# Issue of the key and value pages in a decoder step: two of four pages by ScalarE, two by SyncE

## The chip, the core and the metric

The kernel runs on one core of a Trainium2 chip. The metric is device time in microseconds (us), from the launch of the program to its end, of one execution; the median of several executions is given. Engines are called PE (TensorE, matrix products), DVE (VectorE), ACT (ScalarE), POOL (GpSimd) and SP (SyncE, which only issues DMAs here). Each has its own instruction queue, which it works off in order.

## What is computed

The reference is one inference step of a two-layer hybrid decoder: a prompt of 1024 tokens and 8 samples of 4 new tokens go through the same weights. Each layer runs an SSD scan, a sparse attention and a convolution beside one another, then an output projection, a norm and a gated FFN. The change concerns the attention of the samples. Each sample has 2048 past keys in 16 pages of 128 rows, which lie scattered in a pool and are found through a page table:

```python
def sparse_attend(q, ks, vs, valid):
    s = jnp.einsum('bthd,btkhd->bthk', q, ks).astype(jnp.float32) * HEAD_DIM ** -0.5
    s = jnp.where(valid[:, :, None, :], s, -jnp.inf)
    p = jax.nn.softmax(s, axis=-1).astype(vs.dtype)
    return jnp.einsum('bthk,btkhd->bthd', p, vs)
...
        phys = jnp.take_along_axis(page_table, (pi // PAGE_SIZE).reshape(bsz, -1), axis=1).reshape(idx.shape)
        off = pi % PAGE_SIZE
...
        def pick(cache, new):
            old = cache[phys, layer, off].astype(new.dtype)
            return jnp.where(in_past[..., None, None], old, gather_rows(new, ni))

        return sparse_attend(q, pick(cache_k, k), pick(cache_v, v), valid)
```

The kernel doesn't gather rows. It loads every page of keys and of values, scores all keys, and masks those that the indexer has not chosen.

## The kernel before

Each layer runs the same stages, one after the other: projections and the indexer, the SSD scan with the scoring of the sample's past keys woven into it (the key stage below), the attention of the prompt with the weighing of the sample's past values woven into it (the value stage is its later part), then output projection, norm and FFN. A stage ends with all engines waiting for one another.

**Pages and groups.** 8 samples x 16 pages are 128 pages for keys and as many for values. They are loaded in groups of four pages (one page of each of four samples), `STREAM` = 32 groups a layer for keys and 32 for values. A page is 128 x 256 float32, 128 KB. A group fills one of `NSLOT` = 4 slots of the ring `RING`; the slot's semaphore counts to 64, 16 for each page, and PE waits for all four. The list `LOADS` gives the order in which weights, keys and values go through the four slots.

**Who issues.** `load_pages(eng, layer, name, pages_of_group)` loads, for each page, its number out of the page table into a register of the issuing engine's sequencer (L424) and issues the DMA (L425). SP walks through `LOADS`; before each it waits until the slot is free (`k_used` or `v_used`, raised by PE after the last product with a group), then calls `load_pages` for its share. Of the first four groups of keys it loads all four pages, of all others pages 0, 1 and 2. ACT loads page 3 of the others, at places written out by hand in its own program:

- in the key stage, `key_tick(k)`: PE turns half a group of keys (two pages, L935) in each tick and scores a group (L947) at the end of each second one; ACT copies each turned half from PSUM into the slot (L1252), and at each odd tick, after its copy, issues the page for the group `k // 2 + 2`. Eight ticks, so four groups, follow in each of eight chunks of the scan; between these bursts lie the scan's own products and the eight exponentials of L1474.
- at the start of the attention stage, for the first four groups of values, before anything else.
- in the value stage: attention runs in pairs of heads, p = 0 to 17. In step p PE makes the scores of pair p (L1084), weighs the three groups of values that `values_of_pair(p)` names (L1159, from p = 7 on), turns the probabilities of the two blocks of pair p - 1 (L1094) and weighs pair p - 2 (L1107). ACT in the same step runs the two exponentials of pair p (L1488), copies the two turned blocks of pair p - 1 (L1252, copy A and copy B below), and then issues the page for each of the groups four further on. DVE masks the scores (L2077) ahead of the exponentials and takes the reciprocal of the sums (L2067) behind them.

In the first pairs, DVE adds the indexer's choice to the sample's scores in turn with PE (L2105 and L1122); these additions stand in DVE's queue between the masks and the reciprocals.

Of the kernel before, what the change touches and what calls it, by code (L numbers as in the profile page):

```python
# [95 lines left out]
NSLOT = 4  # L96
# [82 lines left out]
def build(nc, xT, w_in, w_out, w_up, w_down, vec, ln0, const, pages, cache_k, cache_v, cache_kidx,  # L179
          ssm_in, ssd_in, cc_in, ffn_in, yT, kT_out, v_out, ki_out, ssm_p, ssm_s, ssd_out, cc_out, ffn_out):  # L180
    ctx = ExitStack()
    with ctx:
# [234 lines left out]
        def load_pages(eng, layer, name, pages_of_group):  # L417

            kind, g = name
            cache = {"key": cache_k, "value": cache_v}[kind]  # L420
            w = 256
            for j in pages_of_group:
                at_page = (4 * (g // PAGES) + j) * PAGES + g % PAGES
                page = eng.value_load(PT[0:1, at_page:at_page + 1], min_val=0, max_val=cache_k.shape[0] - 1)  # L424
                eng.dma_start(RING[:, SLOTS[name], j * w:(j + 1) * w], cache[page, layer, :, :]  # L425
                              ).then_inc(loaded[SLOTS[name]], 16)
# [106 lines left out]
        def _(sp):  # L533
# [7 lines left out]
            with sp.Fori(0, DEPTH) as layer:  # L541
# [17 lines left out]
                for n, name in enumerate(LOADS):  # L559
                    kind, slot = name[0], n % NSLOT  # L560
                    if name == ("kidx", 6):
                        sp.wait_ge(stage_done, 4 * 1)
                        store(ki_out[layer, :, :], KID[0:HEAD, :])
                    elif name == ("key", NSLOT):
                        sp.wait_ge(saved, 8)
                        store(ssd_out[layer, :, :, :], SSDO[:, :, :])
                        store(cc_out[layer, :, :, :], CCO[:, :, :])
                        sp.wait_ge(stage_done, 4 * 3)
                        sp.dma_start(HS[:, :, :, :], ssm_in[layer, :, :, :, :]).then_inc(ssm_loaded, 16)
                        for t in range(2):  # L570
                            store(kT_out[layer, t, :, :], KTL[:, t, :])
                        store(v_out[layer, 0:P, 0:NCHUNK, :], VTOK[:, 0:NCHUNK, :])
                        store(v_out[layer, 0:NS, NCHUNK, :], VTOK[0:NS, NCHUNK, :])
                    elif name == ("value", NSLOT):
                        sp.wait_ge(ssd["state"], NCHUNK)
                        store(ssm_p[layer, :, :, :], HP[:, :, :])
                        sp.wait_ge(ssd["state"], NCHUNK + 1)
                        store(ssm_s[layer, :, :, :, :], HS[:, :, :, :])
                    if name == ("up", NSLOT - WHOLE):
                        sp.wait_ge(stage_done, 4 * 5)  # L580
                        for i, j in enumerate(BY_THIRD):
                            sp.dma_start(WOUT[:, i, :], w_out[layer, j, :, :]).then_inc(wout_loaded[i], 16)
                        sp.dma_start(FFO[:, :, FFN_H:], ffn_in[layer, :, :, :]).then_inc(hist_loaded, 16)
                    if n >= NSLOT:
                        old = LOADS[n - NSLOT]
                        if old[0] in ("in", "out", "up", "down"):
                            await_full(sp, JOB[old])
                        elif old[0] == "value":
                            sp.wait_ge(v_used, old[1] + 1)
                        elif old[0] == "key":  # L590
                            sp.wait_ge(k_used, old[1] + 1)
                        else:
                            sp.wait_ge(tr_full, 4 * old[1] + 4)
                    if kind == "kidx":
                        load_index_pages(sp, layer, name[1], 0, 16)
                    elif kind in ("key", "value"):
                        load_pages(sp, layer, name, (0, 1, 2, 3) if kind == "key" and name[1] < NSLOT else (0, 1, 2))
                    elif kind == "in":
                        sp.dma_start(RING[:, slot, 0:KT * P], w_in[layer, name[1], :, :]).then_inc(loaded[slot], 16)
                    elif kind == "out":  # L600
                        sp.dma_start(RING[:, slot, 0:KT * P], w_out[layer, name[1], :, :]).then_inc(loaded[slot], 16)
                    elif kind == "up":
                        sp.dma_start(RING[:, slot, 0:KT * P], w_up[layer, name[1], :, :]).then_inc(loaded[slot], 16)
                    else:
                        first, w = name[1] * FG * P, split_width(name) * P
                        sp.dma_start(RING[:, slot, 0:w], w_down[layer, name[2], :, first:first + w]
                                     ).then_inc(loaded[slot], 16)
# [641 lines left out]
        def _(act):  # L1249
# [85 lines left out]
            with act.Fori(0, DEPTH) as layer:  # L1335
# [112 lines left out]
                def key_tick(k):  # L1448
                    if k < 2 * STREAM:
                        copy_keys(k)  # L1450
                    g = k // 2 - 1
                    if k % 2 and g >= 0 and (g + 1) % 4 == 0 and g < STREAM:
                        quad, q = divmod(g // 4, QUARTERS)
                        act.wait_ge(k_used, g + 1)
                        copy(PAST[quad][:, q * QKEYS:(q + 1) * QKEYS], bank(7)).then_inc(k_kept, 1)
                    if k in FRESH_TICKS:
                        act.wait_ge(k_fresh, FRESH_TICKS.index(k) + 1)
                        copy(FRESH[:, FRESH_TICKS.index(k), :], bank(7, NS)).then_inc(k_kept, 1)
                    ahead = k // 2 + 2
                    if k % 2 and NSLOT <= ahead < STREAM:  # L1460
                        act.wait_ge(k_used, ahead - NSLOT + 1)
                        load_pages(act, layer, ("key", ahead), (3,))

                act.wait_ge(ssd["seg"], 1)
                act.activation(WS[:, 0:NCHUNK, :], WS[:, 0:NCHUNK, :], ACT.Exp)
# [52 lines left out]
                        copy(PRT[0:NS, PAGES, :].rearrange("p (b x) -> p b x", x=16), src).then_inc(smp["copied"], 1)  # L1518

                for g in range(NSLOT):  # L1520
                    load_pages(act, layer, ("value", g), (3,))
                for p in range(len(BLOCKS) // 2 + 1):
                    for n in (2 * p, 2 * p + 1):
                        if n < len(BLOCKS):
                            exp(n)
                    if p == TURNED_AT - 1:
                        exp_sample()
                    for m in turns_of_pair(p):
                        copy_sample(m)
                    if p >= 1:  # L1530
                        copy_turned(2 * p - 2)
                        copy_turned(2 * p - 1)
                    for g in values_of_pair(p):
                        if g + NSLOT < STREAM:
                            act.wait_ge(v_used, g + 1)
                            load_pages(act, layer, ("value", g + NSLOT), (3,))
                stage.end()


# [29 lines left out]
                for m in range(WHOLE, len(SPLIT)):  # L1569
                    name = SPLIT[m]  # L1570
# [869 lines left out]
```

## Time and profile before

| | |
|---|---|
| median of 3 runs | 3820.9 us (3813.37 to 3825.1) |
| the profiled execution | 3816.51 us, its span 3814.7 us |
| busy share PE, DVE, ACT, POOL | 87%, 50%, 32%, 17% |
| key stage, first and second layer | about 586 to 745 and 2460 to 2617 us |
| value stage, first and second layer | about 872 to 981 and 2743 to 2855 us |

Times in the rows are us from the span's start, unless marked ns. A `q` behind an engine (SPq, ACTq) means its sequencer: issuing of DMAs and loads of registers, which don't count as busy time. The chain of work that ended last is followed back from the last instruction, at each step to what released it. The two layers run the same code, and most rows of the first have a counterpart some 1872 us later.

### The profile page before, as it was taken

What the parts mean: (1) busy time and instruction counts of PE and PEld (TensorE: products, weight loads), DVE (VectorE), ACT (ScalarE), POOL (GpSimd) and SP (SyncE); (2) the same over time, 40 slices, a digit from 0 to 9 for tenths busy, and PEclk for the clock granted to TensorE, in tenths of its full rate; (3) what the DMA queues carried; (4) which work ended last, traced back from release to release, by engine and by line L of the source; (5) the groups of instructions that cost most, each with busy time, mean ns of one, the idle gap of its engine ahead of it and who ended that gap; (6) DMA issues with size and microseconds to landing.
All of it is one profiled execution on the core that took longest, in us unless ns stands there. A gap on an engine that the chain in (4) does not pass through costs nothing.

```text
span 3814.7 us, 51646 instructions
## 1 busy us (share of the span) xinstructions
PE 3304.1 (87%) x19286; PEld 2652.2 (70%) x19286; DVE 1909.9 (50%) x2976; ACT 1236.7 (32%) x2251; POOL 638.6 (17%) x651
## 2 busy tenths in 40 slices
PE   4899887857889999999868998786669999999995
PEld 2454455624789999999834453564349899999994
DVE  4467864332475434334435868633226645335335
ACT  3246623333252112212223574243333412112213
POOL 0000000001013333333100000000110333334331
PEclk8999998857999999999989998897589999999998
DMA  3111104304301111111021110142151111111111
GB/s 100 49 36 29 32 17 124 94 17 123 102 17 35 52 48 37 53 50 34 27 81 48 34 34 23 62 117 63 35 155 40 34 45 36 54 45 37 55 34 58
DMA packets 169894, 206.59 MB, mean 54 GB/s; under 512 B 61025, under 2 KB 138146, under 8 KB 168738
## 3 DMA queue, kind: packets, MB, share of 16 engines
q1 hardware_dynamic: 143138, 185.36, 16.4%
q10 hardware_dynamic: 26496, 17.84, 1.6%
q8 instruction: 154, 2.52, 0.3%
q14 instruction: 106, 0.87, 0.1%
HBM read 187.17 MB, written 15.96 MB: 53 GB/s over the span
## 4 chain that ended last, share of the span: by engine, by line
PE 64%; DVE 16%; ACT 9%; SPq 5%; issue 3%; DMA 2%; POOL 0%; ACTq 0%; DVEq 0%; POOLq 0%
PE PS L742 41%; PE PS L723 7%; DVE WORK L1668 4%; DVE MIX L1668 2%; ACT WORK L1435 2%; PE PS L755 2%; PE PS L827 2%; ACT X L1306 2%; SPq L424 2%; SPq L425 2%; DVE WORK L1860 1%; PE PS L935 1%; DMA RING<-cache_k 1%; PE PS L781 1%; DVE WORK L1632 1%
## 5 line engine op out<-in xcount | busy, mean ns | idle before, releaser
L742 PE MATMUL PS<-WORK_parts,WHIGH_parts 128*128 128x352 f32 x4224 | 869.5, 328 | 35.2 <-POOL WORK_parts L709 17.7
L723 PE MATMUL PS<-X,RING 128*128 128x512 f32 (+1 forms) x2016 | 671.8, 496 | 109.3 <-DMA RING<-w_in 65.4
L742 PEld LDWEIGHTS PS<-WORK_parts,WHIGH_parts 128*128 128x128 f32 x4224 | 724.2, 191 | 38.9 <-issue 20.6
L742 PE MATMUL PS<-WORK_parts,RING_parts 128*128 128x352 f32 x3168 | 691.3, 327 | 0.0
L723 PEld LDWEIGHTS PS<-X,RING 128*128 128x128 f32 x2016 | 338.4, 194 | 443.8 <-issue 375.2
L742 PEld LDWEIGHTS PS<-WORK_parts,RING_parts 128*128 128x128 f32 x3168 | 545.4, 190 | 0.0
L1668 DVE SCALAR_TENSOR_TENSOR WORK<-WORK,VEC 128x1072 f32<-128x1072 f32 (+2 forms) x272 | 525.6, 1932 | 9.7
L1252 ACT ACTIVATE WORK<-PS 128x32 f32<-128x32 f32 (+11 forms) x412 | 190.8, 514 | 842.1 <-PE PS L742 579.7
L489 POOL TENSOR_TENSOR RING_parts<-RING,WHIGH_parts 128x1024 fp32r<-128x1024 f32 (+2 forms) x184 | 372.0, 2022 | 467.2 <-ACT WHIGH_parts L1252 466.9
L742 PE MATMUL PS<-X_parts,WHIGH_parts 128*128 128x352 f32 x2016 | 434.4, 323 | 0.0
L1435 ACT ACTIVATE WORK<-WORK 128x512 bf16<-128x512 f32 x310 | 285.7, 922 | 198.5 <-DVE WORK L1907 198.4
L1666 DVE TENSOR_SCALAR WORK<-WORK,VEC 128x1072 f32<-128x1072 f32 (+2 forms) x102 | 80.0, 784 | 529.8 <-ACT WORK L1252 529.4
L742 PEld LDWEIGHTS PS<-X_parts,WHIGH_parts 128*128 128x128 f32 x2016 | 344.4, 188 | 0.0
L1252 ACT ACTIVATE WHIGH_parts<-RING 128x1024 fp32r<-128x1024 f32 (+2 forms) x188 | 155.5, 827 | 442.6 <-PE PS L742 420.0
L2264 DVE TENSOR_TENSOR MIX<-MIX,PS 128x1056 f32<-128x1056 f32 x80 | 100.3, 1253 | 286.9 <-PE PS L742 286.9
L755 PE MATMUL PS<-WORK_parts 128*128 128x352 f32 x576 | 144.2, 330 | 0.0
L2077 DVE CUSTOM_DVE_ANT_0 WORK<-PS,WORK 128x384 f32<-128x384 f32 (+5 forms) x48 | 42.4, 883 | 201.8 <-PE PS L1084 201.8
L709 POOL TENSOR_TENSOR WORK_parts<-WORK,WORK_parts 128x1056 fp32r<-128x1056 f32 x44 | 108.3, 2462 | 167.6 <-ACT WORK_parts L1252 167.6
L1252 ACT ACTIVATE WORK_parts<-WORK 128x1056 fp32r<-128x1056 f32 (+1 forms) x56 | 59.4, 1078 | 217.9 <-DVE WORK L2252 217.9
L935 PE MATMUL PS<-CONST,RING 128*128 128x128 f32 x512 | 83.0, 305 | 49.5 <-DMA RING<-cache_k 30.7
L1860 DVE TENSOR_SCALAR_CACHE_REDUCE WORK<-WORK 128x544 bf16<-128x544 f32 (+6 forms) x164 | 115.9, 742 | 0.3
L935 PEld LDWEIGHTS PS<-CONST,RING 128*128 128x128 f32 x512 | 62.3, 155 | 67.9 <-DMA RING<-cache_k 37.0
(318 smaller groups left out, 3722.2 us busy)
## 6 DMA issues: line engine op xcount, KB each, us to landing
RING<-w_up SPq DMA_DIRECT2D x88, 512.0 KB, 3.6
RING<-cache_k SPq DMA_DIRECT2D x200, 128.0 KB, 2.2
RING<-cache_v SPq DMA_DIRECT2D x192, 128.0 KB, 2.1
RING<-w_in SPq DMA_DIRECT2D x46, 512.0 KB, 3.6
RING<-w_down SPq DMA_DIRECT2D x80, 256.0 KB, 2.7
RING<-cache_v ACTq DMA_DIRECT2D x64, 128.0 KB, 2.5
RING<-cache_k ACTq DMA_DIRECT2D x56, 128.0 KB, 2.6
yT<-X SPq DMA_DIRECT2D x5, 1408.0 KB, 5.5
```

The costliest lines, as they stand in the source:

```text
L489: eng.tensor_tensor(low, raw, WHIGH[:, m % 2, 0:w].bitcast(F32), ALU.subtract).then_inc(done, 1)
L709: pool.tensor_tensor(HIDL[:, b, :], HID[:, b, :], HIDH[:, b, :].bitcast(F32), ALU.subtract).then_inc(hid_low, 1)
L723: mm = pe.matmul(job_psum(n, w, first=first), stationary(k), moving(k)[:, first:first + w], start=k == 0, stop=k == k_tiles - 1)
L742: mm = pe.matmul(thirds(n)[:, third, :], a, x[:, third * THIRD:(third + 1) * THIRD], start=k == 0 and part == 0, stop=k == tiles - 1 and p ...
L755: mm = pe.matmul(dst, a[:, w], third_of(x, t), start=k == 0 and part == 0, stop=k == KT - 1 and part == 2)
L935: mm = pe.transpose(key_bank(k)[:, (j % 2 * 2 + t) * P:(j % 2 * 2 + t + 1) * P], cache_page(name)[:, j, t * P:(t + 1) * P], c("ident"))
L1252: return act.activation(dst, src, ACT.Copy)
L1435: ins = act.activation(SCAN_ASIDE[s][:, 0:w], SEL[:, SEL_AT[i]:SEL_AT[i] + w], ACT.Sign, bias=SCAN_TRIED[:, s:s + 1], scale=SCAN_SCALE, ac ...
L1666: step.then_wait(dve.tensor_scalar(acc, src[:, 0:w], v(col), None, ALU.mult))
L1668: ins = dve.scalar_tensor_tensor(out=acc, in0=src[:, k:k + w], scalar=v(col + k), in1=acc, op0=ALU.mult, op1=ALU.add)
L1860: marks.append(step.mark(dve.tensor_scalar(ASIDE[len(marks) % 2][:, 0:x.shape[-1]], x, limit, None, op, ALU.add, accum_out=to)))
L2264: dve.tensor_tensor(y, y, thirds(n), ALU.add).then_inc(free[n % 2], 1)
```

## The change

SP issues pages 0 and 1 of each group in place of 0, 1 and 2; ACT issues pages 2 and 3 in place of page 3, at the same places of its program. The first four groups of keys stay with SP alone. What is loaded, where to, and what waits for it stay as they are.

```diff
@@ -594,7 +594,7 @@
                     elif kind in ("key", "value"):
-                        load_pages(sp, layer, name, (0, 1, 2, 3) if kind == "key" and name[1] < NSLOT else (0, 1, 2))
+                        load_pages(sp, layer, name, (0, 1, 2, 3) if kind == "key" and name[1] < NSLOT else (0, 1))
@@ -1459,7 +1459,7 @@
                     if k % 2 and NSLOT <= ahead < STREAM:
                         act.wait_ge(k_used, ahead - NSLOT + 1)
-                        load_pages(act, layer, ("key", ahead), (3,))
+                        load_pages(act, layer, ("key", ahead), (2, 3))
@@ -1518,7 +1518,7 @@
                 for g in range(NSLOT):
-                    load_pages(act, layer, ("value", g), (3,))
+                    load_pages(act, layer, ("value", g), (2, 3))
@@ -1533,7 +1533,7 @@
                         if g + NSLOT < STREAM:
                             act.wait_ge(v_used, g + 1)
-                            load_pages(act, layer, ("value", g + NSLOT), (3,))
+                            load_pages(act, layer, ("value", g + NSLOT), (2, 3))
```

## Rows read from the trace of the kernel before

**Rows 1.** The page: its first line, and the engines' shares of the chain.
```profile
span 3814.7 us, 51646 instructions
...
PE 64%; DVE 16%; ACT 9%; SPq 5%; issue 3%; DMA 2%; POOL 0%; ACTq 0%; DVEq 0%; POOLq 0%
```
**Rows 2.** The page's DMA issues: count, KB each, median us from issue to landing.
```profile
RING<-cache_k SPq DMA_DIRECT2D x200, 128.0 KB, 2.2
RING<-cache_v SPq DMA_DIRECT2D x192, 128.0 KB, 2.1
...
RING<-cache_v ACTq DMA_DIRECT2D x64, 128.0 KB, 2.5
RING<-cache_k ACTq DMA_DIRECT2D x56, 128.0 KB, 2.6
```
**Rows 3.** The chain in the first layer's value stage: start, us, what.
```profile
880.23 0.33 SPq L425
...
942.02 0.33 SPq L425
...
964.80 3.06 DMA RING<-cache_v
...
972.62 4.15 DMA RING<-cache_v
```
**Rows 4.** Timeline of PE in one burst of keys: start, us, what, [idle before <-releaser].
```profile
656.44 1.09 PE L935 MATMUL PS<-CONST,RING 128*128 128x128 f32 x8 [2.02 <-DMA RING<-cache_k]
...
658.39 1.09 PE L935 MATMUL PS<-CONST,RING 128*128 128x128 f32 x8 [0.28 <-DMA RING<-cache_k]
```
**Rows 5.** Timeline of ACT in the same burst.
```profile
653.65 0.37 ACTq L425 DMA_DIRECT2D RING<-cache_k  x1
654.07 1.08 ACT L1252 ACTIVATE RING<-PS 128x512 f32<-128x512 f32 x2 [0.58 <-PE PS L935]
654.88 0.36 ACTq L425 DMA_DIRECT2D RING<-cache_k  x1
```
**Rows 6.** Timeline of ACT in the first layer's value stage (L1488 exponential, L1252 copy).
```profile
874.61 0.60 ACT L1252 ACTIVATE WORK<-PS 128x512 f32<-128x512 f32 x1 [0.81 <-PE PS L1094]
...
883.79 0.60 ACT L1252 ACTIVATE WORK<-PS 128x512 f32<-128x512 f32 x1 [3.80 <-PE PS L1094]
885.66 0.60 ACT L1252 ACTIVATE WORK<-PS 128x512 f32<-128x512 f32 x1 [1.27 <-PE PS L1094]
...
890.88 0.83 ACT L1488 ACTIVATE WORK<-WORK 128x640 f32<-128x640 f32 x1 [4.62 <-DVE WORK L2077]
...
895.05 0.70 ACT L1252 ACTIVATE WORK<-PS 128x640 f32<-128x640 f32 x1 [0.92 <-PE PS L1094]
...
950.89 0.92 ACT L1252 ACTIVATE WORK<-PS 128x896 f32<-128x896 f32 x1 [1.91 <-PE PS L1094]
...
957.78 1.16 ACT L1488 ACTIVATE WORK<-WORK 128x1024 f32<-128x1024 f32 x1 [5.96 <-DVE WORK L2077]
...
960.13 1.00 ACT L1252 ACTIVATE WORK<-PS 128x1024 f32<-128x1024 f32 x1
962.73 1.02 ACT L1252 ACTIVATE WORK<-PS 128x1024 f32<-128x1024 f32 x1 [1.60 <-PE PS L1094]
963.49 2.63 ACTq L425 DMA_DIRECT2D RING<-cache_v  x3
...
971.86 1.02 ACT L1252 ACTIVATE WORK<-PS 128x1024 f32<-128x1024 f32 x1 [1.25 <-PE PS L1094]
```
**Rows 7.** Timeline of ACT at the start of the first layer's attention.
```profile
797.46 3.74 ACTq L425 DMA_DIRECT2D RING<-cache_v  x4
...
802.53 0.40 ACT L1488 ACTIVATE WORK<-WORK 128x128 f32<-128x128 f32 x1
```
**Rows 8.** Timeline of DVE at the same place.
```profile
805.59 0.69 DVE L2105 TENSOR_TENSOR WHIGH<-WHIGH,PS 128x512 f32<-128x512 f32 x1 [1.64 <-PE PS L1122]
```
**Rows 9.** Timeline of ACT in the second layer's value stage: first and last copy B.
```profile
2748.78 0.60 ACT L1252 ACTIVATE WORK<-PS 128x512 f32<-128x512 f32 x1 [0.81 <-PE PS L1094]
...
2844.16 1.02 ACT L1252 ACTIVATE WORK<-PS 128x1024 f32<-128x1024 f32 x1 [1.25 <-PE PS L1094]
```

## The prediction, made before the changed kernel was run

> **What bounds the kernel now.** I read the chain of work that ended last first. TensorE carries 64% of it and the issuing of DMAs by SP 5% [rows 1], about 190 us, unusual for an engine that computes nothing. The list of issues says which DMAs those can be: pages of the key and value caches, 200 and 192 on SP, 56 and 64 on ACT, all of 128 KB [rows 2]. The chain in order of time shows where the issuing is late. In the value stage of the first layer SP issues 53 pages from 880.23 to 942.02 us, 61.79/52 = 1.19 us each, and the chain hardly leaves it [rows 3]: three pages a group, 3.6 us a group. There SP's queue sets the pace.
>
> In the key stage the chain runs through SP only in short pieces. Each SSD chunk turns and scores four groups of keys, which I call a, b, c, d. TensorE waits 2.02 us for c at 656.44 and 0.28 us for d at 658.39 [rows 4]. What releases c is ACT's page of it, issued at 653.65 and needed 2.7 us later [rows 4, 5]; what releases d is SP's third page. Seven chunks of each layer, the second to the eighth, repeat this.
>
> **ACT's price.** Where ACT issues three pages in a row it takes 2.63 us from the first to the end of the third, whose own issue is 0.37 long, so (2.63 - 0.37)/2 = 1.13, say 1.14 us, a page [rows 6]: the load of the page number and its checks are in it, and it is as dear as on SP. The change moves 28 key and 32 value pages a layer, 120 in all, 137 us of issuing. SP gives them up, ACT takes them. On ACT they stand in program order between the copies and exponentials that TensorE and VectorE wait for, so everything queued behind them starts later unless it was waiting anyway.
>
> **Keys.** ACT issues its page of c in the tick in which it copies a, and its page of d one tick later; between the two lies 654.88 - 653.65 = 1.23 us, with the copies of b between [rows 5]. With two pages each, c's last page goes at 653.65 + 1.14, d's first at 653.65 + 1.14 + 1.23 = 656.02 and d's last at 657.16. All land about 2.7 us after issue (656.39 - 653.65; the medians of all pages are 2.6 on ACT, 2.2 on SP [rows 2]). So c comes 1.14 us later, plus 0.1 as more pages are in flight; d comes at 659.9 in place of 658.35, 1.5 us later. SP's release is worth nothing here: its third page of d is replaced by one of ACT that goes later still, and its pages for the next chunk are landed before that chunk starts. Per chunk I count 1.5 us where d's landing ended the wait, four of seven in each layer, and 1.2 where TensorE is still busy with c when d comes, three of seven: 8 x 1.5 + 6 x 1.2 = 19.2 us. I take 2 off, since in some chunks a landing was slower than the rest now, and a later issue need not repeat that: 17 us. Ends: 14 (c alone, 1.0 a chunk) and 25 (1.8 a chunk). The other groups' second page, and the copies that it holds back, lie under the 8 us of SSD work between two bursts: nothing, and 1.14 us each if that cover went.
>
> **Start of the attention stage.** ACT first issues one page of each of the first four groups of values, four in 3.74 us from 797.46, and only then the first exponential, at 802.53 [rows 7]. Eight pages put it at 802.53 + 4 x 1.14 = 807.1, its end with the read of the sum at 807.6. VectorE's reciprocal waits for that, and behind the reciprocal in its queue is the addition at 805.59 [rows 8], which now waited for TensorE. It moves to 807.8: 2.2 us, and the additions after it follow one another with TensorE, so the 2.2 stay. Two layers: 4.4 us. Ends: 0 and 2 x 4.56 = 9.1.
>
> **Values.** A step of this stage is, on ACT: two exponentials, copy A, copy B, three groups' pages. From copy B's start to its first page 0.76 us pass (963.49 - 962.73) [rows 6]. Six pages then hold ACT for 0.76 + 5 x 1.14 + 0.37 = 6.83, with the hand-over 6.86 us after copy B began; now it is 3.4. The exponentials were waiting for VectorE's masks until then: they started 5.22 us after copy B at 890.88, and none later than 957.78 - 950.89 = 6.9 [rows 6]. So ACT's slack of up to 3.4 us is used up, and ACT sets the step: 6.86, plus the two exponentials (960.13 - 957.78 = 2.35 at 1024 keys; by their widths 1.75 at 640, mean 2.05), plus copy A to copy B (1.87 in the first of eight steps, 2.60 in the last [rows 6]; all eight add up to 17.5 in the first layer, 18.6 in the second). Eight steps: 8 x (6.86 + 2.05) + 17.5 = 88.8 us. The ninth has no exponentials; its third group needs ACT's fourth page, issued 0.76 + 3 x 1.14 after copy B and landing 2.7 later, at 962.73 + 6.9 = 969.6 in place of SP's 967.86 [rows 3, 6], so it takes 9.13 + 1.7 = 10.8. Together 99.6 against 971.86 - 874.61 = 97.25 now: 2.4 us. The last group's second page adds 1.14 at the very end, where the chain waits for that landing [rows 3]: 3.5 us. The second layer in the same way: 8 x 8.91 + 18.6 + 10.8 = 100.7 against 2844.16 - 2748.78 = 95.38 [rows 9], 5.3 + 1.14 = 6.5 us. Sum 10 us. Ends: 3.9, if all eight pairs of copies take 1.87, and 15.5, if all take 2.60; below nothing in the second rival.
>
> SP's seven remaining microseconds a step are under ACT's; a value group's slot is freed by TensorE as before, and SP no longer is late for it. What SP issues next, the output weights, waits for the same release as now. VectorE's and GpSimd's steps wait for ACT or TensorE and only follow.
>
> **A rule of the skill.** What the rows say is that 1.19 us of issuing stands against 2.2 us to landing, and that SP is on the chain for 60 us [rows 2, 3]. The Trainium skill, "DMA: Bandwidth & Descriptors", section "Issuing engines are not separate DMA queues", says that issuing from several engines saves only the sequencer's time, which is usually small beside the DMA. Here the trace does not agree that it is small. By that rule nothing would move and the time would stay at 3821; this stands as a rival below.
>
> **The sum.** 17 + 4.4 + 10 = 31.4 us. The profiled execution took 3816.5 us, of which 3814.7 is its span [rows 1]; with the change 3847.9. It lies 4.4 below the median of the runs, 3820.9, to which the same sum gives 3852.
>
> **The rivals.** First, not slower: SP's queue is the bound of the value stage and ACT's pages stay hidden there. It decides at 6.86 us after copy B: if the masks come later than that, ACT's issuing costs nothing. Steps as short as 895.05 - 885.66 = 9.4 occur now [rows 6]; at 9.6 eight steps take 76.8 instead of 88.1, 22.6 us less over two layers. With 21.4 for the other two places this ends at 3821 - 1 = 3820. Against it: most masks come before 6.86 already. 10%. Second, the same with the keys' pages hidden as well, as would be if c and d waited for SP alone: 3820.9 - 22.6 + 4.4 = 3803; the row at 656.44 speaks against it. 4%. Third, slower still: pages of both queues, issued in step, delay one another. The last value page took 4.15 us to land [rows 3]; were all last pages of c and d as late, 1.4 us more in 14 chunks, 20 us, give 3872. Most land in 2.7. 9%. Fourth, issuing is small and nothing moves: 3821. 3%; the 53 pages in the chain speak against it.
>
> **How the numbers follow.** My forecast, 3852, has 74%. Its own range, from the low ends (14 + 0 + 3.9 = 18) to the high ones (25 + 9.1 + 15.5 = 50), is 3839 to 3871. The range to be given reaches down towards the first rival and up to the third: 3828 to 3873. A measurement of this kernel can tell about 0.3%, 11.5 us, from no change. Slower by more than that: forecast and third rival, 0.83; within: first and fourth, 0.13; faster: the second, 0.04.
>
> **What would show it.** In the key stage TensorE's waits for c and d should end with ACT's pages, and the chunk be 1.2 to 1.5 us longer; the first exponential of attention should follow eight issues, some 4.6 us later; in the value stage SP should have gaps and the chain go through ACT's issuing, with steps of 10.2 to 12 us. Steps under 10 us with exponentials that still wait for VectorE would make me wrong, and so would a wait for c that ends no later than now.

## The result and the profile after

The changed kernel takes 3859.19 us (median of four runs, 3856.02 to 3862.72) against 3819.99 us for the kernel before, measured beside it (four runs, 3813.37 to 3825.1): a ratio of 1.0105 with a 95% interval of 1.0088 to 1.0122, or 39.2 us more. The profiled execution of the changed kernel took 3857.0 us, that of the kernel before 3816.5, so 40.5 us more are to be found in the two traces.

Three parts of the page of the changed kernel answer to rows 1 and 2: its head, the chain by engine, and the issues of pages.

```profile
span 3855.2 us, 51646 instructions
...
PE 64%; DVE 16%; ACT 10%; issue 3%; ACTq 3%; DMA 2%; SPq 2%; POOL 0%; DVEq 0%; POOLq 0%
...
RING<-cache_k SPq DMA_DIRECT2D x144, 128.0 KB, 2.6
RING<-cache_v SPq DMA_DIRECT2D x128, 128.0 KB, 2.3
RING<-cache_v ACTq DMA_DIRECT2D x128, 128.0 KB, 2.1
RING<-cache_k ACTq DMA_DIRECT2D x112, 128.0 KB, 2.9
```

The change did what it says: 144 and 128 pages from SP, 112 and 128 from ACT. SP's issuing falls from 5% of the chain to 2%, and ACT's rises from 0% to 3%. Nothing was won by the exchange. Where the 40.5 us went is read best by cutting both traces at the same instructions: the key stage from the first chunk's exponentials (L1474) to the ninth's, the start of attention from the first product of L1122 to the first L1502, the value stage from the first L1159 to the first L1192.

| us, first + second layer | before | after | more | predicted |
|---|---|---|---|---|
| key stage | 146.2 + 144.6 | 157.8 + 157.9 | 24.9 | 17 |
| start of attention | 34.8 + 34.8 | 38.1 + 38.0 | 6.5 | 4.4 |
| value stage | 110.0 + 111.5 | 113.3 + 113.9 | 5.7 | 10 |
| all else | 3232.8 | 3236.2 | 3.4 | 0 |

**Key stage.** TensorE's timeline in the changed kernel, in the burst that answers to rows 4 (us of the start, us from first to last, what it is, how often, and in brackets the idle time before it and what ended that):

```profile
655.61 1.09 PE L935 MATMUL PS<-CONST,RING 128*128 128x128 f32 x8
656.64 0.64 PE L947 MATMUL PS<-RING,WORK 128*32 128x128 f32 x16
660.72 1.86 PE L935 MATMUL PS<-CONST,RING 128*128 128x128 f32 x8 [3.44 <-DMA RING<-cache_k]
662.51 1.08 PE L947 MATMUL PS<-RING,WORK 128*32 128x128 f32 x16
663.52 1.45 PE L935 MATMUL PS<-CONST,RING 128*128 128x128 f32 x8
664.90 0.64 PE L947 MATMUL PS<-RING,WORK 128*32 128x128 f32 x16
```

The wait for c is 3.44 us, where rows 4 have 2.02. Two more things are to be seen. There is no wait for d any more: d's products at 663.52 follow c's at once. And the products behind the wait are slow: c's eight turns take 1.86 us, those ahead of the wait 1.09. The chain of the changed kernel says what the wait hung on (start, duration, link; the last link ahead of the wait is the landing of ACT's second page of c):

```profile
656.51 0.37 ACTq L425
...
657.67 3.00 DMA RING<-cache_k
...
660.72 1.86 PE PS L935 x8
```

Over the whole key stage of the first layer, the two groups of TensorE's matmuls that the pages feed, first in the kernel before and then in the changed one (count, busy us, mean ns of one, then the idle time before them by what ended it):

```profile
L935 PE MATMUL PS<-CONST,RING 128*128 128x128 f32 x256 | 41.9, 307 | 24.9 <-DMA RING<-cache_k 15.5 <-ACT WORK L1476 9.3
L947 PE MATMUL PS<-RING,WORK 128*32 128x128 f32 x512 | 23.0, 303 | 0.5 <-ACT WORK L1252 0.5
```

```profile
L935 PE MATMUL PS<-CONST,RING 128*128 128x128 f32 x256 | 45.3, 325 | 31.0 <-DMA RING<-cache_k 21.5 <-ACT WORK L1476 9.3
L947 PE MATMUL PS<-RING,WORK 128*32 128x128 f32 x512 | 24.3, 317 | 1.6 <-ACT WORK L1252 1.6
```

Waits for pages grew by 21.5 - 15.5 = 6.0 us, waits for ACT's copies by 1.1, and the products themselves by 3.4 + 1.3 = 4.7 us although they are the same products. Together that is 11.8 us, and the stage grew by 11.6: it is accounted for.

**Value stage.** The shares of the chain by engine and line over most of this stage answer to rows 3; first in the kernel before (875 to 966 us), then in the changed one (892 to 985 us):

```profile
by line: SPq L425 30.4%; SPq L424 29.7%; issue 17.9%; DMA RING<-cache_v 9.3%; PE PS L1094 3.8%; PE PS L1159 3.5%; PE PS L1107 3.5%; PE PS L1084 2.7%; ACT WORK L1252 1.0%; ACTq L424 0.2%; ACTq L425 0.2%
```

```profile
by line: ACTq L425 18.4%; ACTq L424 16.6%; issue 14.1%; DMA RING<-cache_v 12.0%; PE PS L1094 11.6%; ACT WORK L1488 10.6%; ACT WORK L1252 8.3%; PE PS L1159 4.6%; PE PS L1084 3.4%; PE PS L1107 2.4%; ACTq L1496 0.1%
```

SP had 60% of this chain and has none of it now; ACT's issuing has 35%, its exponentials and copies 19%. SP, which issued a page every 1.19 us in the kernel before (rows 3), now waits for a free slot in nine places of this stage (waits of SP's queue, 889 to 996 us: total, count, longest):

```profile
SPq L424 <- PE PS L1159: 31.7, 9, 6.0
```

One step of ACT in the changed kernel, to be held against rows 6:

```profile
923.03 0.70 ACT L1252 ACTIVATE WORK<-PS 128x640 f32<-128x640 f32 x1 [0.92 <-PE PS L1094]
923.79 6.06 ACTq L425 DMA_DIRECT2D RING<-cache_v  x6
929.90 0.94 ACT L1488 ACTIVATE WORK<-WORK 128x768 f32<-128x768 f32 x1 [6.16 <-DVE WORK L2077]
```

Copy B starts at 923.03, the exponential at 929.90, 0.05 us behind the sixth issue. The bracket names VectorE's mask, since an issue is not counted as work; but in all eight steps of this layer the first exponential starts 0.05 to 0.06 us behind the sixth issue, whatever the bracket names, so it is the issues that hold it.

### The profile page after: what moved, and what is told of

Its sections match the earlier page's. It is cut to its first block, busy times and chain, and to the rows that moved or that the text cites. A ratio compares the mean times of both kernels' runs of the same rounds, so it can differ in the third digit from the quotient of the medians.

```text
span 3855.2 us, 51646 instructions
## 1 busy us (share of the span) xinstructions
PE 3321.4 (86%) x19286; PEld 2663.4 (69%) x19286; DVE 1910.1 (50%) x2976; ACT 1235.2 (32%) x2251; POOL 639.4 (17%) x651
## 4 chain that ended last, share of the span: by engine, by line
PE 64%; DVE 16%; ACT 10%; issue 3%; ACTq 3%; DMA 2%; SPq 2%; POOL 0%; DVEq 0%; POOLq 0%
PE PS L742 40%; PE PS L723 7%; DVE WORK L1668 4%; DVE MIX L1668 2%; PE PS L755 2%; ACT WORK L1435 2%; PE PS L827 2%; ACT X L1306 2%; PE PS L935 2%; ACTq L425 1%; ACTq L424 1%; DVE WORK L1860 1%; ACT WORK L1252 1%; DMA RING<-cache_k 1%; PE PS L1094 1%
## 5 line engine op out<-in xcount | busy, mean ns | idle before, releaser
L742 PEld LDWEIGHTS PS<-WORK_parts,WHIGH_parts 128*128 128x128 f32 x4224 | 724.1, 191 | 38.9 <-issue 20.6
L1252 ACT ACTIVATE WORK<-PS 128x32 f32<-128x32 f32 (+11 forms) x412 | 190.6, 513 | 825.4 <-PE PS L742 581.2
L1252 ACT ACTIVATE WHIGH_parts<-RING 128x1024 fp32r<-128x1024 f32 (+2 forms) x188 | 155.5, 827 | 437.9 <-PE PS L742 418.9
L935 PE MATMUL PS<-CONST,RING 128*128 128x128 f32 x512 | 91.3, 327 | 61.0 <-DMA RING<-cache_k 42.0
L1252 ACT ACTIVATE WORK_parts<-WORK 128x1056 fp32r<-128x1056 f32 (+1 forms) x56 | 59.4, 1078 | 217.7 <-DVE WORK L2252 217.7
L935 PEld LDWEIGHTS PS<-CONST,RING 128*128 128x128 f32 x512 | 69.2, 168 | 80.5 <-DMA RING<-cache_k 47.8
```

What stands on the lines that cost most here:

```text
L742: mm = pe.matmul(thirds(n)[:, third, :], a, x[:, third * THIRD:(third + 1) * THIRD], start=k == 0 and part == 0, stop=k == tiles - 1 and p ...
L935: mm = pe.transpose(key_bank(k)[:, (j % 2 * 2 + t) * P:(j % 2 * 2 + t + 1) * P], cache_page(name)[:, j, t * P:(t + 1) * P], c("ident"))
L1252: return act.activation(dst, src, ACT.Copy)
```

## The experiments

In most of these kernels one new line says which pages ACT issues, and SP issues the rest; ACT's three calls and SP's one take their pages from it:

```diff
+        def acts_pages(kind, g):
+            return () if kind == "key" and g < NSLOT else ...
-    load_pages(sp, layer, name, (0, 1, 2, 3) if kind == "key" and name[1] < NSLOT else (0, 1, 2))
+    load_pages(sp, layer, name, [j for j in range(4) if j not in acts_pages(*name)])
-    load_pages(act, layer, ("key", ahead), (3,))
+    load_pages(act, layer, ("key", ahead), acts_pages("key", ahead))
```

Only what stands behind that `else`, and what else was changed, is shown below. These kernels' rows name lines that are three further on (L938 is L935, L950 L947, L1255 L1252, L1477 and L1479 L1474 and L1476, L1491 L1488).

### One part of the change at a time

The change for the keys alone:

```diff
+ (2, 3) if kind == "key" else (3,)
```

> The change for the keys alone; values stay with three pages on SP and one on ACT. My theory (the costs of the three places add up, and the key stage has most of them): the key stage grows as in the changed kernel, from 146 to about 158 us a layer, and the time goes up by 24 to 26 us, some 0.65%; the value stage stays as before. The rival (the keys hardly matter, and the loss comes from ACT's exponentials in attention): within 6 us of before.

Measured: 3858.92 us against 3824.5, ratio 1.0097 (1.0058 to 1.0136). The key stages took 157.9 + 157.9 us, those of the full change to 0.1 us, so 25 us belong to the keys whatever the values do. The median moved by 34.4; its profiled execution's span grew by 38.2, of which 25.0 lie in the key stages, 1.6 in the value stages and some 11.5 in stretches whose code is the same in both kernels. The last of these can only be scatter between executions.

The change for the values alone:

```diff
+ (3,) if kind == "key" else (2, 3)
```

> The change for the values alone, both at the start of attention and in the value stage. My theory: 3.3 us a layer at the start of attention and 1.5 to 4 us a layer in the value stage, so 10 to 14 us above before, with steps of the value stage that go exponential, exponential, copy, copy, six issues without a gap on ACT. The rival (SP's queue was the bound, and its release pays): the value stage 10 us a layer shorter, the time 10 to 20 us under before.

Measured: 3841.0 us, ratio 1.0042 (1.0025 to 1.0060), 16.5 us more. Start of attention 38.4 + 38.3, value stages 113.6 + 116.0, keys 147.2 + 143.4: 7.1 us from the start and 8.1 from the value stage, where 10 to 14 in all were expected. The values cost too, by themselves.

Two pages of the first four groups of values alone, and one of all others:

```diff
+ (2, 3) if kind == "value" and g < NSLOT else (3,)
```

> ACT issues two pages of each of the first four groups of values; all others as before. Theory: the first exponential comes 4.6 us later, and 3.3 us of it stay (the addition behind VectorE's reciprocal moves by 2.2, and more where it pushes the next): start of attention 38.1 us in place of 34.8, 6.6 us in all; nothing elsewhere. The rival (later waits take the delay up): under 2 us in all.

Measured in one run: 3832.07 us. The start took 38.4 + 37.3 us, 6.1 more than before, with ACT's eight issues ahead of its first exponential:

```profile
799.97 8.60 ACTq L428 DMA_DIRECT2D RING<-cache_v  x8
...
809.89 0.40 ACT L1491 ACTIVATE WORK<-WORK 128x128 f32<-128x128 f32 x1
```

So the growth of the start comes from these eight issues and not from what follows. All four kernels with the eight issues have 37.3 to 38.4 us here. The others have 34.7 to 36.1, but four of them 30.9 or 31.0 in the second layer with the same code, which stays unexplained: against those the start's loss is larger than 3.3 us a layer. The value stages of this kernel, 113.6 + 107.2, lie on both sides of those before though their code is the same: a single value stage can be read to some 3 us only. The fourteen value stages of this study with three pages on SP and one on ACT from the fifth group on took 107.2 to 113.6 us, 110.7 in the mean, and the six with two and two 113.3 to 116.0, 114.0 in the mean.

### Which landing costs in the key stage

Two pages of c alone, and then of d alone:

```diff
+ (2, 3) if kind == "key" and g % 4 == 2 else (3,)
```

> ACT issues two pages of the third group of each burst (c) alone; all other groups as before. Theory 1 (the longer wait for c is what counts: TensorE idles long enough in each burst that its granted clock falls to half, and the turns of c then run at half clock): almost all of the key stage's growth is here, 9 to 12 us a layer, bursts of 20.4 us throughout, granted clock 0.83 in each burst. Theory 2 (my prediction: c and d each count by their own landing, and the clock has no part): 1.2 us in each of seven chunks, 8 us a layer at most, with bursts of 19 us where they were 17.8.

```diff
+ (2, 3) if kind == "key" and g % 4 == 3 else (3,)
```

> ACT issues two pages of the fourth group of each burst (d) alone; all other groups as before. Theory 1 (the wait for c and the clock are what counts): d's last page goes 2.37 us after c's instead of SP's third 2.33 us after it, so its landing moves by 0.1 to 0.5 us and the key stage by 0 to 3 us a layer. Theory 2 (d's landing costs 1.5 us in four of seven chunks): 6 us a layer.

Measured, one run each: 3849.83 us with c, 3832.34 with d. Key stages 158.0 + 157.6 with c, which is all that the full change costs there; 150.6 + 151.9 with d, 4.4 + 7.3 more than before. TensorE's rows in a burst with c alone, and then with d alone:

```profile
663.80 1.91 PE L938 MATMUL PS<-CONST,RING 128*128 128x128 f32 x8 [3.50 <-DMA RING<-cache_k]
...
666.65 1.40 PE L938 MATMUL PS<-CONST,RING 128*128 128x128 f32 x8
```

```profile
681.00 1.09 PE L938 MATMUL PS<-CONST,RING 128*128 128x128 f32 x8 [0.78 <-DMA RING<-cache_k]
...
683.91 1.09 PE L938 MATMUL PS<-CONST,RING 128*128 128x128 f32 x8 [1.24 <-DMA RING<-cache_k]
```

A later page of d does cost, some 6 us a layer, when c is early, as Theory 2 had it. With c late as well it costs nothing more: 12.4 us a layer for c, 5.9 for d, and 12.5 for both. The lateness of c and its slow products take longer than d's landing needs, so d's is covered: in the changed kernel's burst above d's last page landed at 662.97 and d's turns began at 663.52. For c, Theory 1 held. These are two single executions, but fourteen bursts in each.

### The place or the number of issues

Two pages on ACT as in the change, but each key group issued one odd tick earlier, a whole group ahead:

```diff
+ (2, 3) if kind == "key" else (3,)
-                    ahead = k // 2 + 2
+                    ahead = k // 2 + 3
```

> Two pages of each group of keys on ACT as in the changed kernel, but issued one group earlier (for the group k // 2 + 3): c's pages at the end of the burst before, d's in the first odd tick. Values as before. Theory (not the number of pages on ACT costs, but that c's pages are issued inside its own burst, where TensorE then idles and its clock falls): c no longer waits, d's four pages go two by two from both queues and land about 4 us after the release in place of 4.7; bursts of 16.5 to 17.5 us at full clock, the key stage 6 to 15 us a layer shorter than before. The rival (ACT's issuing time as such costs, by holding back its copies): the key stage stays longer than before, 5 to 12 us a layer.

The same with one page:

```diff
+ (3,)
-                    ahead = k // 2 + 2
+                    ahead = k // 2 + 3
```

> As before, three pages on SP and one on ACT, but ACT's page of keys issued one group earlier. Theory: the wait for c goes, d still waits for SP's third page, 4.7 us after the release: bursts of 17.8 us where they were that, and less than 19 to 20.6 where the clock had fallen; 0 to 8 us a layer. The rival (ACT's page was not what c waited for): no change.

Measured: 3810.7 us with two pages, ratio 0.9978 (0.9964 to 0.9992), and 3811.89 in one run with one page. Key stages 142.0 + 141.5 (most chunks 17.8 us) and 143.0 + 142.3, 7.3 and 5.5 us shorter than before, 32 and 30 shorter than with the change. The same number of issues costs 25 us in one place and nothing in another, so it is the place that counts in the key stage. What is left to wait for is something else (rows of a burst with two early pages, then the group of turns in its first key stage):

```profile
639.41 1.07 PE L938 MATMUL PS<-CONST,RING 128*128 128x128 f32 x8 [1.57 <-ACT RING L1255]
...
641.75 1.06 PE L938 MATMUL PS<-CONST,RING 128*128 128x128 f32 x8 [0.71 <-ACT RING L1255]
...
L938 PE MATMUL PS<-CONST,RING 128*128 128x128 f32 x256 | 38.5, 290 | 25.1 <-ACT RING L1255 14.6 <-ACT WORK L1479 9.3 <-DMA RING<-cache_k 1.2
```

Waits for pages are down from 15.5 us to 1.2, but 14.6 us of waits for ACT's copies have come up, because two issues stand ahead of the copy of the next half. The rival view, that ACT's issues cost by holding back its copies, is right in kind for this kernel; it was not what cost in the changed one, where such waits are 1.6 us in all. With one early page these waits are 3.1 us and those for pages 13.0; c then waits for no page in any burst of the first layer (at most 0.41 us for a copy of ACT's), and what is left is nearly all d's wait for SP's pages. So ACT's page was what c waited for in the kernel before, as the prediction said.

### What the granted clock adds

In the changed kernel the products behind the wait are slow. This kernel is the changed one with 20 transposes of the identity put ahead of TensorE's wait for c, into a bank that is overwritten after. Since the bank must be free for them, the wait for ACT's copy out of it now stands ahead of the wait for the pages, in every tick:

```diff
+                    if k >= 2:
+                        pe.wait_ge(k_copied, k - 1)
+                    if half == 0 and g % 4 == 2 and g >= NSLOT:
+                        for _ in range(20):
+                            pe.transpose(key_bank(k)[:, 0:P], c("ident"), c("ident"))
                     if half == 0:
                         pe.wait_ge(loaded[SLOTS[name]], ARRIVED[name])
-                    if k >= 2:
-                        pe.wait_ge(k_copied, k - 1)
```

> The changed kernel, with 20 transposes of the identity on TensorE just before it waits for c's pages; they write into the bank that c's own transposes then overwrite, add nothing to the output, and fill 3 of the 3.4 us of waiting. Theory (the later c costs 1.4 us, and the rest of a burst's growth is that TensorE idles, its granted clock falls to half, and c's and d's products run at it): granted clock 1.00 in the bursts, eight turns in 1.1 us and not 1.9, bursts of 18.8 to 19.5 us where they were 20.5, the key stage 6 to 10 us a layer shorter than in the changed kernel. The rival (the products are slow for another reason, the clock has no part): bursts of 20.5 us or longer.

Measured in one run: 3850.22 us, key stages 153.6 + 153.0. Stretches of such bursts, the changed kernel first, then the one with transposes (length; busy us of PE, its weight load, DVE, ACT, POOL; granted clock; share of the DMA engines, GB/s):

```profile
656.00:666.00 10.00, 6.56 (x81) 5.01 (x81) 0.26 (x1) 3.36 (x7) 0.00 (x0) 0.83 0.46 133
655.00:669.00 14.00, 10.56 (x132) 7.74 (x131) 1.85 (x5) 4.56 (x8) 0.00 (x0) 0.88 0.48 140
```

```profile
655.00:669.00 14.00, 10.84 (x144) 8.38 (x146) 1.89 (x3) 5.96 (x13) 0.00 (x0) 1.00 0.43 125
```

```profile
660.45 2.40 PE L931 MATMUL PS<-CONST 128*128 128x128 f32 x20 [1.48 <-ACT RING L1255]
662.81 1.09 PE L938 MATMUL PS<-CONST,RING 128*128 128x128 f32 x8
...
664.99 1.06 PE L938 MATMUL PS<-CONST,RING 128*128 128x128 f32 x8 [0.51 <-DMA RING<-cache_k]
```

With work in the wait the granted clock stays at 1.00 and c's turns take 1.04 to 1.09 us in all fourteen bursts of the two layers, where the changed kernel has 1.45 to 1.97. So the slow products are a consequence of TensorE's idling ahead of them. But the burst got only 0.6 to 0.7 us shorter (19.9 against 20.5 from chunk to chunk, between what the theory and the rival had), and the two stages 4.2 + 4.9 where I had expected 6 to 10 each. TensorE's rows for the key stage of the first layer, to be held against those of the changed kernel above (L931 is the transposes), say where the rest went:

```profile
L938 PE MATMUL PS<-CONST,RING 128*128 128x128 f32 x256 | 37.3, 284 | 14.0 <-ACT WORK L1479 9.3 <-DMA RING<-cache_k 4.4 <-ACT RING L1255 0.2
L950 PE MATMUL PS<-RING,WORK 128*32 128x128 f32 x512 | 21.3, 286 | 1.6 <-ACT WORK L1255 1.6
L931 PE MATMUL PS<-CONST 128*128 128x128 f32 x140 | 16.8, 275 | 7.7 <-ACT RING L1255 7.7
```

The same products take 58.6 us in place of 69.6, so 11.0 are given back. But TensorE now waits 3.9 us for d over the seven bursts, where it waited for none: in the burst shown d's last page lands at 664.85, 6.65 us after ACT's first issue for c at 658.20 (6.25 in the prediction). And the time ahead of c, idle and transposes together, is 25.0 us in place of 21.5: in thirteen of the fourteen bursts the transposes end 0.09 to 1.3 us after c's last page has landed, and so they hold c up themselves, by 1.7 us over this layer's seven. The experiment, one execution, shows the cause of the slow products; what the clock costs in time it understates, by up to that. With c late, the order of events that the prediction had, d ending the wait, is there only at full clock.

### Who bounds the value stage

Two pages on ACT for one group in three, so eight pages a step on SP and four on ACT, between nine and three before and six and six after:

```diff
+ (2, 3) if kind == "value" and g >= NSLOT and g % 3 == 1 else (3,)
```

> Two pages on ACT for each third group of values from the fifth on, one for the others and for all keys: a step then has eight pages on SP and four on ACT. Theory (two queues, each the bound past its slack): SP needs 8 x 1.17 = 9.4 us a step, ACT is free 0.76 + 3 x 1.14 + 0.37 = 4.6 us after copy B, before most masks; the value stage 2 to 9 us a layer shorter than before. The rival (a step is bound by TensorE, the clock and the copies and not by SP): within 2 us a layer.

Measured: 3800.19 us against 3819.96, ratio 0.9949 (0.9931 to 0.9967). Value stages 101.4 + 99.4 us, 8.6 and 12.1 shorter than before. ACT in one of its steps:

```profile
901.25 0.70 ACT L1255 ACTIVATE WORK<-PS 128x640 f32<-128x640 f32 x1 [0.92 <-PE PS L1097]
902.01 3.78 ACTq L428 DMA_DIRECT2D RING<-cache_v  x4
905.85 0.94 ACT L1491 ACTIVATE WORK<-WORK 128x768 f32<-128x768 f32 x1 [3.89 <-DVE WORK L2080]
```

The exponential comes 4.6 us after copy B; in the four later steps of this layer it comes after 5.0 to 6.0, when ACT's issues are done and something else is waited for. So SP's queue was the bound before, as the chain said, and moving issues to ACT does gain; nine to three is too many on SP, six to six too many on ACT, and the gain lies between; seven to five was not tried. The Trainium skill, "DMA: Bandwidth & Descriptors", section "Issuing engines are not separate DMA queues", has it that issuing on several engines at once saves only the time that the sequencer takes to initiate a DMA, usually small beside the DMA itself. Here it is not small: an issue takes 1.14 to 1.19 us against 2 to 3 us from issue to landing, and one page in twelve moved to ACT is worth 19.8 us.

### Both together

Pages one group early, two of them on ACT for every d and for one group of values in three:

```diff
+ (2, 3) if kind == "value" and g >= NSLOT and g % 3 == 1 or kind == "key" and g % 4 == 3 else (3,)
-                    ahead = k // 2 + 2
+                    ahead = k // 2 + 3
```

> A version meant to be faster: ACT's pages of keys one group earlier, two of them for d alone and one for the others, and for values two pages on ACT in each third group. If the gains of the two places add up (3 to 4 us a layer in the key stage, 8 to 12 in the value stage): 24 to 32 us under before.

And with two pages on ACT for all keys:

```diff
+ (2, 3) if kind == "key" or g >= NSLOT and g % 3 == 1 else (3,)
-                    ahead = k // 2 + 2
+                    ahead = k // 2 + 3
```

> As the last, with two pages on ACT for every group of keys (from the fifth on), one group earlier. If the gains add up: 24 to 32 us under before. It may be 1 us a chunk longer than the last, since ACT issues two pages before it can copy b.

Measured: 3795.87 us against 3819.25, ratio 0.9930 (0.9904 to 0.9956), and 3799.08, ratio 0.9945 (0.9927 to 0.9964). The first is the shortest median of all these kernels, 23.4 us under the kernel before, the second is 20.2 under it: both less than expected, and hardly more than the values alone gave (19.8), from which the intervals do not set them apart. The key stages of the first are 138.8 + 137.6 us, 14.4 shorter than before; its value stages 108.8 + 101.3, only 11.4 shorter where the third alone gave 20.7. The second has 142.2 + 141.8 and 103.9 + 107.4, so 6.8 and 10.2 shorter than before; its key stages are 7.6 us longer than the first's, about 0.5 us a chunk and not 1. The code of the value stage is the same in all three, and its six readings go from 99.4 to 108.8 us, 103.7 in the mean. What sets them apart stays open.

## Why the prediction was right, point by point

The sum was 31.4 us and the traces differ by 40.5. The direction, the three places and ACT's price of an issue held, and so did the rule of the value stage's step. In the key stage, over half of the sum, the last step of the mechanism did not: c's landing and TensorE's clock cost the time, not d's landing. One end term had the wrong sign. Against their predictions keys, start and all else are 7.9, 2.1 and 3.4 us over and the values 4.3 under; that the misses partly cancel, and that the keys just stay inside their range, is luck.

- **What bounds the kernel**: confirmed in both places, by the chain of the value stage and the eight-to-four split, which gained, and for the keys by ACT's page issued early, after which c no longer waits for pages.
- **ACT's price of 1.14 us a page**: confirmed. Six issues take 6.06 us, five spaces and 0.37, so 1.14; eight took 8.30 and 8.60, which makes 1.13 and 1.18.
- **Keys, 17 us predicted, 24.9 measured**, at the upper end of 25. The step that failed is the one that counted 1.5 us a chunk by d's landing. In the changed kernel d is never waited for. What costs is c: its last page was issued 1.1 us later and took 3.0 us to land instead of 2.7 (the 0.1 that the prediction allowed for more pages in flight was 0.3), which makes the wait 1.4 us longer (3.44 against 2.02); and then TensorE's clock, for which the sum had no term, added 4.7 us in the first layer. The 2 us taken off because a late issue need not repeat a slow landing went the wrong way too: pages on ACT's queue took 2.9 us in the median, not 2.6. In which chunks it fell shows the same: of those from the second to the seventh in the first layer, the one that took 20.6 us before takes 20.6 now, and the five others, 17.8 to 19.5, now take 20.5 to 21.5. The one that was slow already had no more to lose. The sign of this stood in the trace of the kernel before. The three chunks of seven in which the prediction found TensorE "still busy with c when d comes" are those in which c's turns took 1.79 to 1.97 us and not 1.09, two of them behind waits no longer than that of rows 4 (1.94 us, and 2.00 in this row of the kernel before):

```profile
692.12 1.94 PE L935 MATMUL PS<-CONST,RING 128*128 128x128 f32 x8 [2.00 <-DMA RING<-cache_k]
```

- **Nothing for the other groups' second page**: nearly so. 1.1 us a layer of waits for copies, against nothing.
- **Start, 4.4 us predicted, 6.5 measured**. The steps are there: first exponential 9.62 us after the first issue where it was 5.07 (4.55 later, 4.56 predicted), and in VectorE's timeline the addition right behind the late reciprocal:

```profile
817.61 0.16 DVE L2067 RECIPROCAL WORK<-WORK 128x1 f32<-128x1 f32 x1 [3.73 <-ACT WORK L1488]
817.69 0.67 DVE L2105 TENSOR_TENSOR WHIGH<-WHIGH,PS 128x512 f32<-128x512 f32 x1
...
823.64 0.69 DVE L2105 TENSOR_TENSOR WHIGH<-WHIGH,PS 128x512 f32<-128x512 f32 x1 [2.23 <-PE PS L1122]
```

From the first issue of each kernel that addition moved by 2.10 us (2.2 predicted), the next by 2.09, and the one at 823.64 by 3.05: there VectorE waits 2.23 us for TensorE instead of 1.28. The step that failed is "the additions after it follow one another with TensorE, so the 2.2 stay". TensorE's two products for it took 2.05 us in place of 1.10, at a granted clock of 0.50 in 820 to 827 us where the kernel before had 0.78 in 808 to 814 (VectorE's addition and TensorE's products before, then the products after):

```profile
810.59 0.69 DVE L2105 TENSOR_TENSOR WHIGH<-WHIGH,PS 128x512 f32<-128x512 f32 x1 [1.28 <-PE PS L1122]
809.46 1.10 PE L1122 MATMUL PS<-WORK 128*128 128x512 f32 x2 [1.07 <-DVE WORK L2098]
...
821.55 2.05 PE L1122 MATMUL PS<-WORK 128*128 128x512 f32 x2 [1.07 <-DVE WORK L2098]
```

The same term was missing as for the keys. That the later exponential brought the clock down here is what the rows suggest (TensorE waited 2.13 us ahead of the products before these, where it did not wait in the kernel before, and 1.07 ahead of these in both); it was not tried by itself.
- **Values, 10 us predicted, 5.7 measured**. The rule of the step was right to the tenth: 6.87 us from copy B to the exponential against 6.86; nine steps of 99.7 us in the first layer against 99.6, of 102.1 in the second against 100.7. In the second layer the ninth took 13.2 instead of 10.8, since TensorE waited 2.12 and 2.14 us for two of its groups; the eight before took 88.9 (89.9 predicted). That is 9.2 us for the steps, 7.7 predicted. The stretches ahead of the first copy B, 1.7 us longer in the first layer and 1.5 shorter in the second, all but cancel. The step that failed is "the last group's second page adds 1.14 at the very end". There the stage got shorter, by 0.9 us and 2.8 us, although the page was issued later:

```profile
984.75 2.10 DMA RING<-cache_v
...
992.76 2.16 DMA RING<-cache_v
994.96 0.62 PE PS L1159 x8
```

The last page landed in 2.16 us where rows 3 have 4.15. Before, SP's first transfers of output weights, 512 KB each, were issued within 0.6 us of that page; now SP has slack and had issued them 5 and 7 us ahead of it, at 985.90 and 987.73. The transfers' price shows again in the second layer before, where the last page took 4.36 us with a transfer issued 0.15 us ahead of it, and in the changed kernel's first layer: the two pages issued 0.3 us behind the one transfer and 0.4 ahead of the other took 3.88 and 5.29 us. That they share the DMA engines is what the times suggest; it was not tried by itself. The 4.15 of rows 3 was, by these rows, a price of that company, and no ground for adding 1.14 to it.
- **All else, nothing predicted, 3.4 us measured.** It lies in the stretch between the value stage of the first layer and the key stage of the second, 1487.9 us before and 1493.0 after. Over the kernels of this study, whose code is one and the same there, it took 1487.1 to 1496.5, so the difference is within the scatter. Single runs of parts therefore don't add to the microsecond.
- **The rivals.** That masks hide ACT's issuing in the value stage fell with the values' part alone (3841 us, slower) and with the steps of the changed kernel, where the issues end last; that the keys are hidden fell with the keys' part alone (3859, slower). The third, pages that delay one another, is partly true: 2.9 us in place of 2.6 in the median for ACT's pages of keys, 3.0 for c's last in the burst shown (2.7 to 3.5 in all fourteen), not the 4.15 that it was priced at. That nothing moves fell with the result.

## What to carry to other kernels

Where an engine that computes also issues DMAs, count the issues into its in-order program like any other instruction, and ask of each place how much slack stands behind it: here 25 us were lost by issuing a second page just ahead of the need, and nothing by the same issue one group earlier. A queue that bounds a stage should be relieved only until the other queue's slack is used up, and the split that fits comes from the two per-step sums (of the three splits tried here, eight to four and not nine to three or six to six). And a wait that gets longer on TensorE is not the end of the bill: look at the duration of the matmuls behind the wait, not at the wait alone, and look for it in the kernel before as well.

## What the runs showed of the hardware

**TensorE's granted clock fell behind its waits.** In the kernel before, the burst with the wait of 2.02 us for c kept a granted clock of 1.00, and another, with a wait of 2.00, had 0.83 (rows of the kernel before, columns as above):

```profile
653.00:662.00 9.00, 6.70 (x100) 4.92 (x98) 0.40 (x1) 3.74 (x7) 0.00 (x0) 1.00 0.52 151
689.00:699.00 10.00, 8.00 (x97) 5.78 (x95) 0.09 (x1) 3.55 (x7) 0.00 (x0) 0.83 0.52 143
```

So the length of that one wait did not decide it: of the fourteen bursts of the kernel before, eight kept c's turns at 1.09 us, behind waits of 0.65 to 2.05 us, and six did not, behind waits of 1.94 to 3.55. With the change all fourteen have slow turns, behind waits of 0.84 to 3.67, and the granted clock of the five that I read is 0.83 over 10 us. The mean mixes the two levels, 2.4 GHz and 1.2 GHz: turns behind the wait take 1.86 us, ahead of it 1.09. With transposes in the wait it stayed at 1.00. Beside a burst that had kept its clock, 1.4 us more of waiting so came with about 1.5 us of slower work: 0.77 in c's turns, 0.44 in its scoring (1.08 against 0.64), 0.36 in d's turns (1.45 against 1.09).

**A page's landing depends on what stands beside it.** 128 KB took 2.10 and 2.16 us where no 512 KB transfer was issued within 0.7 us of it, 3.00 as the second of two pages in a row on ACT while SP issued as well, and 4.15 and 4.36 beside the 512 KB transfers at the end of the value stages of the kernel before.

**An issue with a page number loaded for it costs nearly the same on both sequencers**: 1.14 us on ACT, 1.15 to 1.18 on SP within a run of pages (1.19 with the steps between groups), against a DMA instruction that itself is 0.34 to 0.37 us long; the rest is the loading of the number and its checks (the L424 and L425 rows ahead of it in the chain). By that price 28 pages of keys a layer are 32 us of ACT's time, but moving the seven pages of c alone cost as much as moving all 28.
